# Attention of a two-path streaming encoder: split (high and low) operands against plain float32, one head norm for nine query tiles, and a longer queue from scores to values

## The reference, cut to what matters

```python
def diff_attn_core(q, k, v, qpos, kpos, lam):
    s = jnp.einsum('bqhcd,bkhcd->bchqk', q.astype(jnp.float32), k.astype(jnp.float32)) * (HD_B ** -0.5)
    allowed = (kpos[None, :] // CHUNK) <= (qpos[:, None] // CHUNK)
    p = jax.nn.softmax(jnp.where(allowed, s, NEG_INF), axis=-1)
    w = p[:, 0] - lam * p[:, 1]
    return jnp.einsum('bhqk,bkhe->bqhe', w, v.astype(jnp.float32))
...
    o = rmsnorm(o, g_sub.reshape(H_B, 2 * HD_B)) * (1.0 - lam_init)
    return o.reshape(bsz, seqlen, V_B).astype(xn.dtype) @ w_o
```

## Time and profile before

| | |
|---|---|
| median of 3 runs | 3091.3 us (3089.08 to 3093.0) |
| span of the profiled execution | 3083.9 us; its time outside the span is not recorded |
| busy PE, DVE, ACT, POOL | 92%, 47%, 26%, 13% of the span |
| attention loop, first scores to last transposed output | 1638 to 2151.5 us |
| mean granted clock of PE | 0.925 of 2.4 GHz |

### The profile page before, as it was taken

One profiled execution on the slowest core, in us unless ns is written; L12 is line 12 of the kernel. 1 busy time (PEld: TensorE's weight loads), 2 busy tenths in 40 slices (PEclk: granted clock), 3 DMA queues, 4 the chain that ended last, 5 costly groups with the idle time before them and its releaser, 6 DMA issues.

```text
span 3083.9 us, 45377 instructions
## 1 busy us (share of the span) xinstructions
PE 2849.6 (92%) x17589; PEld 2757.6 (89%) x17589; DVE 1437.7 (47%) x2364; ACT 788.6 (26%) x1511; POOL 413.4 (13%) x503
## 2 busy tenths in 40 slices
PE   7998998699999999978998999888969999999995
PEld 6998988699999999977997888777969999999995
DVE  5324655653333333364217666665374333333345
ACT  4103442221111111132115444443131111111122
POOL 0000000231100111112001121111032111001111
PEclk8998998899999999988998788775989999999997
DMA  3325442011111111112322111111101111111111
GB/s 110 98 91 128 113 114 59 27 42 42 48 48 41 48 48 42 47 34 72 109 77 69 47 49 45 35 60 40 41 14 48 49 46 42 48 44 45 48 41 56
DMA packets 252103, 177.50 MB, mean 58 GB/s; under 512 B 14153, under 2 KB 241953, under 8 KB 252017
## 3 DMA queue, kind: packets, MB, share of 16 engines
q1 hardware_dynamic: 171152, 109.57, 11.8%
q10 hardware_dynamic: 80864, 66.77, 7.3%
HBM read 141.59 MB, written 34.66 MB: 57 GB/s over the span
## 4 chain that ended last, share of the span: by engine, by line
PE 65%; issue 20%; DVE 8%; ACT 3%; POOL 3%; SPq 0%; DMA 0%; ACTq 0%; POOLq 0%; DVEq 0%
PE PS L329 21%; PE PS L330 20%; PE PS L331 20%; DVE X L1531 2%; DVE XL L1229 1%; DVE Y L1527 1%; PE PS L380 1%; ACT P L1132 1%; POOL AS L1822 1%; POOL AS L1819 1%; DVE AS L1696 1%; PE PS L369 0%; PE PS L627 0%; ACT TH L1151 0%; DVE P L1680 0%
## 5 line engine op out<-in xcount | busy, mean ns | idle before, releaser
L329 PE MATMUL PS<-XH,WH 128*128 128x352 f32 x3072 | 1017.6, 331 | 75.6 <-DVE XL L1229 62.6
L330 PE MATMUL PS<-XL,WH 128*128 128x352 f32 x3072 | 999.7, 325 | 0.0
L331 PE MATMUL PS<-XH,WL 128*128 128x352 f32 x3072 | 999.0, 325 | 0.0
L329 PEld LDWEIGHTS PS<-XH,WH 128*128 128x128 f32 x3072 | 588.9, 192 | 87.1 <-issue 48.0
L330 PEld LDWEIGHTS PS<-XL,WH 128*128 128x128 f32 x3072 | 590.4, 192 | 0.0
L331 PEld LDWEIGHTS PS<-XH,WL 128*128 128x128 f32 x3072 | 588.0, 191 | 0.0
L329 PE MATMUL PS<-HH,WH 128*128 128x352 f32 x1536 | 500.3, 326 | 4.8 <-DVE WL L1202 4.8
L331 PE MATMUL PS<-HH,WL 128*128 128x352 f32 x1536 | 499.0, 325 | 0.0
L330 PE MATMUL PS<-HL,WH 128*128 128x352 f32 x1536 | 496.7, 323 | 0.0
L736 ACT ACTIVATE WH<-WR 128x1024 fp32r<-128x1024 f32 x192 | 202.0, 1052 | 773.5 <-PE PS L331 588.8
L1584 DVE TENSOR_TENSOR Y<-Y,PS 128x352 f32<-128x352 f32 x384 | 199.6, 520 | 397.7 <-PE PS L331 396.7
(11 more groups left out here) (239 smaller groups left out, 2977.5 us busy)
## 6 DMA issues: line engine op xcount, KB each, us to landing
WR<-in_w_up SPq DMA_DIRECT2D x64, 512.0 KB, 4.0
WR<-in_w_down SPq DMA_DIRECT2D x64, 512.0 KB, 3.4
proj_s<-STG ACTq DMA_DIRECT2D x24, 528.0 KB, 2.7
WR<-in_w_in_a SPq DMA_DIRECT2D x24, 512.0 KB, 3.8
CH<-proj_s ACTq DMA_DIRECT2D x8, 1024.0 KB, 11.8
WR<-in_w_kv SPq DMA_DIRECT2D x16, 512.0 KB, 3.9
out<-OT ACTq DMA_DIRECT2D x16, 512.0 KB, 3.3
OG<-proj_s ACTq DMA_DIRECT2D x8, 528.0 KB, 3.8
```

The source lines that it names most:

```text
L329: pe.matmul(out, lh, rh, start=start, stop=False)
L330: pe.matmul(out, lh, rl, start=False, stop=False)
L331: return pe.matmul(out, ll, rh, start=False, stop=stop)
```

## The change

Queries, keys, values and turned weights are used as they are, in plain float32: one matmul where there were three, and no high and low parts (all `split_k`, `split_q`, the V splits, `att_turned_lo` and POOL's part are gone). The mask matmul is plain float32 too. Keys, values and queries have two buffers by head and are loaded by DMA straight to where PE reads them. P0 has three buffers, P1 two. The PE transposes tile t-2 and multiplies tile t-3 (before t-1 and t-2), and DVE combines t-1 at the end of its step, after both maxima. ACT copies the turned weights first in its step, then makes both exponentials.

The norm over a head's 128 output channels is made once for nine tiles: outputs stay unscaled in OC, ACT squares all nine tiles in one instruction (step 3 of the next head), DVE reduces (step 4), POOL takes one power, DVE multiplies nine tiles at once (step 5), and PE turns them in steps 6, 7 and 8 in rounds of 4, 4 and 1 tiles through the same PSUM bank as the values, so the values of those steps wait for ACT's copy. The last head's norm runs behind blocks 0 to 2 of the output projection, its transposes stand behind blocks 3 to 5.

```diff
+            KK = sb("KK", [P, 2, NKEY], F32, sc)
+            VV = sb("VV", [P, 2, 13, P], F32, sc)
+            QQ = sb("QQ", [P, 2, T], F32, sc)
+            P0 = sb("P0", [P, 3, D], F32, sc)
+            P1 = sb("P1", [P, 2, D], F32, sc)
+            TT = sb("TT", [P, 2, KB, P], F32, sc)
+            OC = sb("OC", [P, 2, NCH, P], F32, sc)
...
 def att_scores (PE)
-                        pe.matmul(out, QH[r, t.hp, qs], kh, start=True, stop=False)
-                        if not t.sample and c + w == t.keys:
-                            pe.matmul(PS[t.f, t.bank(m, c), w - P:w], MA[r, :], MB[r, :], start=False, stop=False,
-                                      skip_group_check=True)
-                        pe.matmul(out, QH[r, t.hp, qs], kl, start=False, stop=False)
-                        mm = pe.matmul(out, QL[r, t.hp, qs], kh, start=False, stop=True)
+                        masked = not t.sample and c + w == t.keys
+                        mm = pe.matmul(PS[t.f, t.bank(m, c), 0:w], q, KK[r, t.hp, t.k0 + c:t.k0 + c + w],
+                                       start=True, stop=not masked, skip_group_check=True)
+                        if masked:
+                            mm = pe.matmul(PS[t.f, t.bank(m, c), w - P:w], MA[r, :], MB[r, :], start=False, stop=True,
+                                           skip_group_check=True)
...
 def att_values (PE)
-                    mm = three(PS[t.f, 6, 0:P], TH[k, t.par, b, t.f], TL[k, t.par, b, t.f], VH[k, t.v0 + b, :],
-                               VL[k, t.v0 + b, :], b == 0, b == len(t.blocks) - 1)
+                    mm = pe.matmul(PS[t.f, 6, 0:P], TT[0:K, t.par, b, t.f], VV[0:K, t.hp, t.v0 + b, :],
+                                   start=b == 0, stop=b == len(t.blocks) - 1)
...
 PE, one step
                     if m < TPT:
                         att_scores(t, first)
-                    if m - 1 < TPT and not (first and m < 1):
-                        att_turn(Tile(q, m - 1))
-                    if not (first and m < 4):
-                        att_out(Tile(q, m - 4), m - 4 == TPT - 1)
+                    if m - 2 < TPT and not (first and m < 2):
+                        att_turn(Tile(q, m - 2))
+                    if m < TPT and t.i in OUT_ROUND and not (first and t.hp == 0):
+                        att_out(t.h - 1, 1 - t.hp, OUT_ROUND.index(t.i), t.n - 3)
...
+                    if not (first and m < 3):
+                        o = Tile(q, m - 3)
+                        if m < TPT and t.i in OUT_ROUND and not (first and t.hp == 0):
+                            pe.wait_ge(sem("a_otc"), 3 * t.h + (OUT_ROUND.index(t.i) - 2))
+                        att_values(o, first)
...
+            def out_behind(k):
+                if 3 <= k < 6:
+                    att_out(H - 1, 1, k - 3, TPT * NPAIR)
...
 ACT, one step
+                    if m - 2 < TPT and not (first and m < 2):
+                        att_turned(Tile(q, m - 2), first)
+                    ...att_out(t.h - 1, OUT_ROUND.index(t.i), OTS) in steps 6, 7, 8
                     if m < TPT:
                         att_exp(t, 0, first)
-                    if not (first and m < 4):
-                        att_take_out(Tile(q, m - 4), first, last and m >= 4)
-                    if m - 1 < TPT and not (first and m < 1):
-                        att_turned_hi(Tile(q, m - 1), first)
                         att_exp(t, 1, first)
-                    if m - 3 < TPT and not (first and m < 3):
-                        att_sumsq(Tile(q, m - 3))
                         att_extras(q, t, first, last)
...
+            def att_square(h, hp):
+                act.wait_ge(sem("a_oc"), 9 * h + 9)
+                act.wait_ge(sem("a_ss"), h)
+                act.activation(SQS[:, :, :], OC[:, hp, :, :], ACT.Square).then_inc(sem("a_sq"), 1)
...
 DVE, one step
-                        att_combine(Tile(q, m - 1))
-                        att_take(Tile(q, m - 3))
-                        att_norm(Tile(q, m - 4))
+                        att_take(Tile(q, m - 4))
                         att_max(t, 0)
+                        att_share(Tile(q, m - 1))
                         att_max(t, 1)
-                        att_turned_lo(Tile(q, m - 1))
+                        att_combine(Tile(q, m - 1))
+                        att_extras(q, t, first, last)
...
+            def att_variance(h, hp):
+                s0 = SM[:, hp, 0, :]
+                dve.scalar_tensor_tensor(HS[:, 1, :], s0, EPS, s0, ALU.mult, ALU.mult)
+                dve.wait_ge(sem("a_sq"), h + 1)
+                dve.reduce_sum(HS[:, 0, :], SQS[:, :, :], AX).then_inc(sem("a_ss"), 1)
+                dve.wait_ge(sem("a_ss"), h + 1)
+                dve.scalar_tensor_tensor(HS[:, 2, :], HS[:, 0, :], 1.0 / P, HS[:, 1, :], ALU.mult, ALU.add)\
+                    .then_inc(sem("a_var"), 1)
+
+            def att_norm(h, hp):
+                dve.wait_ge(sem("a_pow"), h + 1)
+                dve.tensor_tensor(OC[:, hp, :, :], OC[:, hp, :, :], HS[:, 3, :].unsqueeze(2).to_broadcast([P, NCH, P]),
+                                  ALU.mult).then_inc(sem("a_on"), 1)
```

More of the change, by code:

```diff
@@ L362, in first_pair @@
                                 mm.then_inc(mm_done, 1)
+                    if behind is not None:
+                        behind(k)
             def token_sums(name):
@@ L1125, in att_exp @@
             def att_exp(t, m, first):
                 act.wait_ge(sem("a_max"), 2 * t.n + (m + 1))
-                if m == 0 and not (first and t.n < 2):
-                    act.wait_ge(sem("a_turned"), t.n - 1)
-                if m == 1:
-                    act.wait_ge(sem("a_comb"), t.n)
-                dst = P0[t.f, t.par, 0:t.keys] if m == 0 else P1[t.f, 0:t.keys]
-                act.activation(dst, t.score(m), ACT.Exp, bias=t.number(m),
-                               accum_out=t.number(4 + m)).then_inc(sem("a_exp"), 1)
@@ L1146, in att_turned_hi, with att_out @@
-            def att_turned_hi(t, first):
+                if m == 0 and not (first and t.n < 3):
+                    act.wait_ge(sem("a_turned"), t.n - 2)
+                if m == 1 and not (first and t.n < 2):
+                    act.wait_ge(sem("a_comb"), t.n - 1)
+                act.activation(t.first_map() if m == 0 else t.second_map(), t.score(m), ACT.Exp, bias=t.number(m),
+                               accum_out=t.total(m)).then_inc(sem("a_exp"), 1)
+            def att_out(h, r, dst):
+                act.wait_ge(sem("a_oT"), 3 * h + (r + 1))
+                c = slice(512 * r, min(512 * r + 512, T))
+                act.activation(dst[:, c], PS[:, 6, 0:c.stop - c.start], ACT.Copy).then_inc(sem("a_otc"), 1)
@@ L1656, in att_extras @@
                     split_lo(t.hp, 2 * q + (U_Q + t.hp + 3))
-                if t.i == 1:
-                    dve.wait_ge(sem("v_hi"), h + 1)
-                    lower(VL[:, 0:NT, :], VR[:, 0:NT, :], VH[:, 0:NT, :]).then_inc(sem("v_lo"), 1)
-                if t.i == 8 and more:
-                    split_k(h + 2)
-                if t.i in SPLIT and more:
-                    split_q(h + 1, (t.hp + 1) % 2, SPLIT.index(t.i))
-                if not more and 1 <= t.i < H:
+                if t.i == 4 and not (first and t.hp == 0):
+                    att_variance(h - 1, 1 - t.hp)
@@ L1665, in att_extras @@
+                if t.i == 5 and not (first and t.hp == 0):
+                    att_norm(h - 1, 1 - t.hp)
+                if not more and 1 <= t.i < H - 1:
                     x_lo(t.i - 1, "sub", "wo")
@@ L1829, in _, with att_pow, att_turn_of_loop @@
+            def att_pow(h):
+                pool.wait_ge(sem("a_var"), h + 1)
+                pool.tensor_tensor(HS[:, 3, :], HS[:, 2, :], half[:, :], ALU.pow).then_inc(sem("a_pow"), 1)
+            def att_turn_of_loop(q, first=False):
+                for hp in range(2):
+                    if not (first and hp == 0):
+                        att_pow(2 * q + (hp - 1))
             att_turn_of_loop(0, first=True)
```

310 lines of the change are left out of this document (116 added, 194 removed).

## The result

| | before | after |
|---|---|---|
| median of 4 runs, us | 3091.36 (3089.08 to 3093.0) | 2967.31 (2966.61 to 2969.65) |
| span of the profiled execution, us | 3083.9 | 2964.8 |
| mean granted clock | 0.925 | 0.958 |

What follows compares the result with a forecast made beforehand. The prediction took PE's work and its clock to bound the kernel before; 94 us off heads 0 to 6 and 35 off the last head and tail made 129, so 3091.3 us became 2962, range 2925 to 3045.

Steps and rivals of the forecast that it cites:

- The kernel after, PE at full clock, 47.5 us a head: Attention heads: 42.5 us of PE work plus 5.0 us of waits, if the clock holds.
- Values, 0.34 to 0.22 us a block, 4.9 us saved: Value matmuls, 41 blocks a head: one plain matmul has two stationary loads instead of three, saving 4.9 us a head.
- Scores +2.0 us: Score matmuls: 64 units of 0.22 us, 14.1 us a head in plain float32 against 12.1 before, so 2.0 lost.
- The 1.28 us wait goes: PE's wait for DVE's combination after the sample tile's scores disappears, since combination and transposes come a step later.
- R's chain: Experiments' theory, not the prediction's: a closed chain through DVE and ACT sets each step; 8.37 us read in tile 7.
- DVE near 32 us, ACT under 29: Busy time per head: DVE falls from 42 to about 32 us, ACT below its 29, both under PE's 42.5.
- Heads 0 to 6, 94 us gained: First seven heads: from 425.7 us to 7 x 47.5 - 1 = 331.5 us, 94 us less.
- Last head and tail, 35 us gained: Last head and its tail: 52 us taken, between 45 at full clock and 70 at the lower level; 35 us gained.
- PE, taking its work in order, sets the end; no other engine is near: Kernel before, attention heads: 61.5 us is 45.2 of PE work, about 11 from the low clock, some 5 of waiting.
- Rival E: Attention: no gain, as the chain maximum, exponential, scores gets longer; 61 us a head, about 3090 us; chance 0.03.
- The low clock adds 11 us a head: Kernel before, heads: 23.9 us of each period at 1.2 GHz add about 11 us to 45.2 us of PE work.
- rival A: The forecast itself: clock stays at the upper level from step 2 of head 0 on, 2962 us; chance 0.60.

Runs made afterwards that it cites:

- the last step of the series: Head norm left out too, against the kernel before with plain float32 values and scores and no low parts: 2983.87 us, ratio 0.9662 to the kernel before.

## Why the prediction was right, and where its reasons were not

- **The kernel after, PE at full clock, 47.5 us a head:** right, 47.3 to 47.4 in four heads (head 1: 48.0; head 4: 48.9). Two terms were off and cancelled, which was luck. PE's work is 44.7 us by its busy time, not 42.5: plain values saved less and plain scores cost more than forecast, as said below. The waits are 2.7 us, not 5.0, and stand ahead of values and not of the scores behind steps 7 and 8; the exponentials were not late.
- **Values, 0.34 to 0.22 us a block, 4.9 us saved:** the price is right, 0.22 from block to block (the 0.22 had been the mean of 0.30 us for a matmul of 128 columns and 0.14 for one of a single column). The saving is about 3 us: 13.4 us a head before, counted at full clock, and 10.3 after for the 41 blocks. The start of each tile's values was left out, and the sample tile was priced like the others, though its stationary operand has 32 columns: there PE's starts are 0.11 us apart even at 1.2 GHz (0.21 for 128 columns).

```profile
1827.44 0.31 PE L330 MATMUL PS<-VL,TH 128*32 128x128 f32 x1
1827.55 0.31 PE L331 MATMUL PS<-VH,TL 128*32 128x128 f32 x1
```

  So a block of the sample tile costs 0.16 us split at full clock (0.32 at 1.2 GHz, halved) and 0.22 plain. The four passes of the Trainium skill, page "FP8 and Floating Point Precision", section TensorE Precision Notes, would have given 0.45 us for the other blocks. The trace does not agree there: two weight loads instead of three decide at 128 stationary columns. For the sample tile, where the load is short, 0.16 to 0.22 is near the four thirds of that page of the Trainium skill.
- **Scores +2.0 us:** in the kernel after +2.8 (13.5 to 16.3). The sum of 64 units left out the start of each tile, 0.2 to 0.3 us, and put the sample tile at 4 units (0.88 us) where it has two pieces a map; it takes 1.33. The difference goes with the mask's second record and the order of the maps: plain scores with a split mask are 13.0, and with both maps issued piece by piece 12.9.
- **The 1.28 us wait goes:** right, but all that the distance gave together was 12.7 us (R's chain, shorter by the order of combination and maxima, included).
- **DVE near 32 us, ACT under 29:** 29.4 and 22.8.
- **Heads 0 to 6, 94 us gained:** 97.1. Heads 1 to 6 took 286.3 us for 285 forecast; head 0 took 42.2 for 46.5, where the forecast had put it only 1 us below the others.
- **Last head and tail, 35 us gained:** 24.6. This term of the sum was mis-sized: 52 us were taken between 45 (full clock) and 70, and it is 63.0, with 30.7 us of it at the lower clock. With the clock kept up for most of it, it was 55.5, so the clock is about 7.5 of the missing 11 us; the other 3.5 are open. The norm's chain hid as said; the last head's turned outputs stand among the projection's matmuls without a wait ahead of them:

```profile
2043.81 0.60 PE L659 MATMUL PS<-ident,OC 128*128 128x128 f32 x4
2047.13 0.60 PE L659 MATMUL PS<-ident,OC 128*128 128x128 f32 x4
2050.52 0.24 PE L659 MATMUL PS<-ident,OC 32*128 32x32 f32 x1
```

- **"PE, taking its work in order, sets the end; no other engine is near":** wrong of the kernel before. Taking 7.0 us of a head off PE's busy time shortened the head by 2.0 us; taking work off DVE, ACT and POOL alone shortened it by 5.1 and 6.9 more. Rival E had a chain of this kind in mind, at a chance of 0.03, but only its part through maxima, exponentials and scores; the low parts and the norm in it were not costed. The savings on DVE and ACT, of which it said that they "cost nothing while PE runs" and so put at nothing, were where the gain came from: low parts and norm gave 78 of the heads' 97 us, in that order of taking. The share of busy time hid it, since DVE (42 us) and ACT (29 us) largely take turns: each alone looks idle, but together they are 71 us in a head of 61.5. The sum came out all the same because these savings turned PE into the engine that holds the kernel.
- **The low clock adds 11 us a head:** as arithmetic on PE's time it stands, as time of the kernel it does not: with plain values the clock rose from 0.80 to 0.87 and the head lost 2 us. The clock was held by the change (rival A was right of that), and plain values did much of it (0.87 with plain values alone). But it was a result too: it went from 0.91 to 1.00 when only the norm was taken from DVE and ACT.

So the number came out since the kernel after was costed by its own work and waits, and a kernel held by PE is the one that such a sum fits. That the errors of the terms cancelled was luck. Open: how much of the last step of the series (from 54.6 to 47.7 us) is the shorter ring and how much the clock that rose with it. The run without the norm alone comes nearest (4.5 us less at 0.83), and no run kept the clock low with the whole ring short. In the kernel before, the ring is read instruction by instruction for step 7 alone; for the other steps it rests on the runs.

## What to carry to other kernels

Before calling an engine the bound by its busy share, read one step's wait rows on the others: if two engines wait for each other and neither for the busy one, a ring sets the step, and every small instruction in their queues is on it, whatever its engine's share. Cost the changed kernel by its own resources, engine by engine, and not only by differences; then ask for the ring as well. Once PE is the bound, look at its queue for work that could run side by side: reordering one loop gave 32 us here, a quarter of what the large change gave. And do not read a forecast that hit as proof of its reasons: here the experiments on the kernel before refuted them.

## What the runs showed of the hardware

- Matmuls on the two halves of the rows ran side by side where they stood close in PE's queue. In the changed kernel the second map's first record starts when the first map has three left to start (1766.25 in tile 7, 0.97 us after the first map). With the mask in one record, in the kernel before with plain scores, it also starts with three left, 0.54 us after the first map. Issued alternately they begin 0.14 us apart. The changed kernel with the mask in the split format was not tried.
- Plain float32 and the three split matmuls cost PE nearly the same for scores of up to 512 columns in 64 rows (13.0 and 13.5 us a head). For the values plain float32 is cheaper where the stationary operand has 128 columns (0.34 us a block before, 0.22 after) and dearer where it has 32 (0.16 by estimate before, 0.22 after).
- With two matmuls of 256 columns added to each of six steps of the last head, its stretch at 1.2 GHz fell from 30.7 to 6.8 us, and the head got 7.5 us shorter though it had more to do.
